# Spreading the residual, two buffers for k by token, and the sample softmax between the projections and the first head

## What is computed

```python
k, v = split(x @ kv_w)                         # (T, 16 heads, 64) each
logf = log_sigmoid(x @ f_w + f_b)              # C = cumulative sum of logf
q = x @ q_w
s = q @ k.T * 64 ** -0.5 + C[t] - C[s]         # causal; softmax, then @ v, then @ o_w
# a sample token attends to 512 cached rows (4 pages of 128) and to itself
x = layer_norm(ALPHA * x + y)
```

## Time and profile before

| | us |
|---|---|
| median of 3 runs | 2961.86 (2959.99 to 2962.94) |
| the profiled execution | 2961.01, its span 2959.3 |
| TensorE busy | 2708.5 (92%) |
| VectorE busy | 1109.4 (37%) |
| GpSimd busy | 949.4 (32%) |
| ScalarE busy | 782.5 (26%) |
| mean granted TensorE clock | 0.942 |

### The profile page before, as it was taken

One profiled execution on the slowest core, in us unless ns is written; L12 is line 12 of the kernel. 1 busy time (PEld: TensorE's weight loads), 2 busy tenths in 40 slices (PEclk: granted clock), 3 DMA queues, 4 the chain that ended last, 5 costly groups with the idle time before them and its releaser, 6 DMA issues.

```text
span 2959.3 us, 44731 instructions
## 1 busy us (share of the span) xinstructions
PE 2708.5 (92%) x16907; PEld 2614.2 (88%) x16907; DVE 1109.4 (37%) x2082; ACT 782.5 (26%) x1431; POOL 949.4 (32%) x546
## 2 busy tenths in 40 slices
PE   8999969999999999679995889889799999999994
PEld 8999949999999999479994688779699999999993
DVE  3222372322222223841236555553623222222237
ACT  2111142111111111522222555552421111111114
POOL 2121252111222121622222778861521112121214
PEclk9999969999999999689997899999799999999997
DMA  3111101111111111024668465641011111111111
GB/s 109 50 43 50 44 15 44 43 44 48 53 47 48 45 50 37 15 85 142 211 216 262 125 172 158 172 138 50 22 44 44 44 57 44 50 44 51 44 36 58
DMA packets 203052, 225.83 MB, mean 76 GB/s; under 512 B 13223, under 2 KB 168871, under 8 KB 201884
## 3 DMA queue, kind: packets, MB, share of 16 engines
q1 hardware_dynamic: 194748, 190.40, 21.2%
q0 software_dynamic: 8160, 33.30, 3.6%
HBM read 182.43 MB, written 41.26 MB: 76 GB/s over the span
## 4 chain that ended last, share of the span: by engine, by line
PE 78%; DVE 7%; DMA 4%; POOL 4%; issue 4%; ACT 2%; SPq 1%; POOLq 0%; ACTq 0%; DVEq 0%
PE ps L1703 24%; PE ps L1704 24%; PE ps L1705 24%; POOL ss L812 2%; PE ps L1961 1%; DMA o_t<-oe 1%; DVE ln_t L1365 1%; PE ps L1991 1%; DVE ln_d L1310 1%; DVE ln_t L1369 1%; PE ps L1946 1%; PE ps L1943 1%; POOL xl L697 1%; DMA k_prompt<-ktok 1%; DMA wraw<-kv_w 1%
## 5 line engine op out<-in xcount | busy, mean ns | idle before, releaser
L1703 PE MATMUL ps<-xh,whi 128*128 128x344 f32 x3288 | 1079.0, 328 | 48.5 <-DVE hl L1512 17.6
L1704 PE MATMUL ps<-xl,whi 128*128 128x344 f32 x3288 | 1063.5, 323 | 0.0
L1705 PE MATMUL ps<-xh,wlo 128*128 128x344 f32 x3288 | 1062.9, 323 | 0.0
L650 POOL TENSOR_TENSOR wlo<-wraw,whi 128x1024 fp32r<-128x1024 f32 x197 | 469.6, 2389 | 1681.5 <-ACT whi L867 1681.4
L1703 PEld LDWEIGHTS ps<-xh,whi 128*128 128x128 f32 x3288 | 626.6, 191 | 79.5 <-POOL xl L697 25.5
L1704 PEld LDWEIGHTS ps<-xl,whi 128*128 128x128 f32 x3288 | 629.6, 191 | 0.0
L1705 PEld LDWEIGHTS ps<-xh,wlo 128*128 128x128 f32 x3288 | 629.3, 191 | 0.0
L867 ACT ACTIVATE whi<-wraw 128x1024 fp32r<-128x1024 f32 x197 | 208.1, 1057 | 1137.6 <-DMA wraw<-ffn_w_gu 648.6
L1703 PE MATMUL ps<-zh,whi 128*128 128x344 f32 x1440 | 464.1, 322 | 17.5 <-DVE x L1437 9.5
L1704 PE MATMUL ps<-zl,whi 128*128 128x344 f32 x1440 | 462.4, 321 | 0.0
L1705 PE MATMUL ps<-zh,wlo 128*128 128x344 f32 x1440 | 460.3, 320 | 0.0
(11 more groups left out here) (209 smaller groups left out, 2374.0 us busy)
## 6 DMA issues: line engine op xcount, KB each, us to landing
wraw<-ffn_w_gu SPq DMA_DIRECT2D x88, 512.0 KB, 3.9
wraw<-ffn_w_down SPq DMA_DIRECT2D x44, 512.0 KB, 3.5
kp<-cache_k SPq DMA_DIRECT2D x32, 512.0 KB, 5.5
vp<-cache_v SPq DMA_DIRECT2D x32, 512.0 KB, 3.8
wraw<-a_w_in SPq DMA_DIRECT2D x24, 512.0 KB, 3.8
wraw<-kv_w SPq DMA_DIRECT2D x16, 512.0 KB, 4.0
q_t<-hl POOLq DMA_DIRECT2D x8, 1024.0 KB, 4.7
v_t<-vst POOLq DMA_DIRECT2D x8, 1024.0 KB, 5.6
```

The source lines that it names most:

```text
L650: pool.tensor_tensor(narrow(wlo[:, s, :], cols), narrow(wraw[:, s, :], cols), f32(narrow(whi[:, s, :], cols)), ALU.subtract).then_inc(w_lo, 1)
L1703: pe.matmul(out, w_h, m_h, start=start, stop=False)
L1704: pe.matmul(out, w_h, m_l, start=False, stop=False)
L1705: return pe.matmul(out, w_l, m_h, start=False, stop=stop)
```

## The change

- The residual moves from one piece ahead of `q_low` to four pieces (`residual(it)`), each behind the second `q_low` of iteration 0 to 3. Three small instructions that prepare the samples' own term (qk, even, side) move ahead of iteration 0.
- k by token gets two buffers, ktok[0] and ktok[1] (the second on the place of `hl`, free after the q stores), with a semaphore each.
- On SyncE the order within iteration 4 to 6 becomes: pages of sample 0, next weight 0, pages of sample 1, next weights 1 and 2. The weights of the output projection go behind `load_qk(0, 0)`, which no longer waits for the last stores; `load_qk(0, 1)` waits for all of them.
- On ScalarE `nxt(1)` goes behind `v_tokens` and `nxt(2)` behind the copies of k by token. The high and low parts of the output projection's first three weights go into attention, behind `step(0, 1)` on ScalarE and behind `norm(0, 3)` on GpSimd.
- On VectorE `v_low` of iterations 4 to 7 goes behind the two samples.
- Iteration 7 is written out on TensorE: the scores of the samples are turned between the two `k_turned` into bank 7, the forget values behind them into bank 0, and `sample_weights` goes behind the first `scores`.
- On GpSimd `k_split(0, 0)` goes ahead of the last two k_prompt stores, and the samples' rows are stored after `norm(0, 0)`.

```diff
-        ktok = ka.put("ktok", [P, TB, P], F32)
+        ktok = [ka.put("ktok0", [P, TB, P], F32), Area(ZH_AT + 3 * ROW + TB * P * 4).put("ktok1", [P, TB, P], F32)]
...
             with sp.Fori(KB // 2, KB - 1) as it:
-                load_kvq(it + 1, True)
-                load_samples(it)
-            for m in range(WR):
-                load(SLOTS["o"] + m, SLOTS["o"] + m, w_o[:, :, m * P:(m + 1) * P], used(UNITS["o"] + m))
-            load_samples(KB - 1)
+                load_sample(it, 0)
+                load_kvq(it + 1, 0, True)
+                load_sample(it, 1)
+                load_kvq(it + 1, 1, True)
+                load_kvq(it + 1, 2, True)
+            load_sample(KB - 1, 0)
+            load_sample(KB - 1, 1)
...
-            sp.wait_ge(full[NCH - 1], UNITS["o"])
             sp.wait_ge(kv["res"], 2 * KB)
             sp.wait_ge(kv["qdma"], 16 * KB)
-            sp.wait_ge(kv["vtdma"], 16 * KB)
-            sp.wait_ge(kv["x0dma"], 16 * (KB // 2))
-            sp.wait_ge(kv["x1dma"], 16 * (KB // 2))
+            sp.wait_ge(kv["vtdma"], 16)
+            sp.wait_ge(kv["x0dma"], 16)
+            sp.wait_ge(full[NCH - 1], UNITS["o"])
             load_qk(0, 0)
             load_v(0, 0)
+            for m in range(WR):
+                load(SLOTS["o"] + m, SLOTS["o"] + m, w_o[:, :, m * P:(m + 1) * P], used(UNITS["o"] + m))
+            sp.wait_ge(kv["vtdma"], 16 * KB)
+            for j in range(2):
+                sp.wait_ge(kv[f"x{j}dma"], 16 * (KB // 2))
+                sp.wait_ge(kv[f"k{j}dma"], 16 * (KB // 2))
             sp.wait_ge(kv["kt"], 4 + 2 * KB)
...
-            keys(KB - 1, lambda j: low(SLOTS["o"] + j, SLOTS["o"] + j))
...
-            pool.dma_start(a["v_sample"].rearrange("b t h d -> b (t h d)"), stok[:, 0, :]).then_inc(kv["s3dma"], 16)
-            pool.dma_start(a["k_sample"].rearrange("b t h d -> b (t h d)"), stok[:, 1, :]).then_inc(kv["s3dma"], 16)
+            store_v(KB - 1)
...
             k_split(0, 0)
+            store_ktok(KB - 1, 0)
+            store_ktok(KB - 1, 1)
             norm(0, 0)
+            sample_rows_out()
             k_split(0, 1)
             for st in range(1, STEPS):
                 norm(0, st)
+            for m in range(WR):
+                low(SLOTS["o"] + m, SLOTS["o"] + m)
...
-                    nxt(1 + j)
                     if j == 0:
                         v_tokens(it)
+                        nxt(1)
                 for j in range(2):
                     if keys:
-                        x = 2 * it + j - KB
-                        if not (isinstance(x, int) and x == 0):
-                            act.wait_ge(kv["kdma"], 16 * x)
-                        by_token(ktok, 5 - 2 * j, kv["kt"], kv["ktok"], 2 * x + 4)
+                        k_tokens(it, j)
+                nxt(2)
+
+            def k_tokens(it, j):
+
+                x = 2 * it + j - KB
+                if isinstance(it, int) and it == KB // 2:
+                    act.wait_ge(kv["qdma"], 16 * KB)
+                else:
+                    act.wait_ge(kv[f"k{j}dma"], 16 * (it - KB // 2))
+                by_token(ktok[j], 5 - 2 * j, kv["kt"], kv["ktok"], 2 * x + 4)
 
             def nxt_slots(it):
                 g = g0 + 3 * it
...
-            kvq(KB - 1, True, nxt_slots(KB - 1))
+            act.wait_ge(kv["vt"], 2 * KB)
+            take(g0 + 3 * (KB - 1), stage[0], 0, KB - 1, 1.0, kv["v"])
+            take_k(KB - 1, 0)
+            v_tokens(KB - 1)
+            take_k(KB - 1, 1)
+            act.wait_ge(sm["tsc"], 1)
+            act.activation(sst[:, 0:NPAST], ps[:, 7, :], ACT.Copy).then_inc(sm["sst"], 1)
+            for j in range(2):
+                k_tokens(KB - 1, j)
 
...
-            act.wait_ge(kv["s3dma"], 16 * 2)
+            act.wait_ge(kv["vtdma"], 16 * KB)
+            for j in range(2):
+                act.wait_ge(kv[f"k{j}dma"], 16 * (KB // 2))
...
             dve.tensor_tensor_scan(fr[:, 0:TP], fz[:, 0:TP], fz[:, 0:TP], 0.0, ALU.add, ALU.bypass).then_inc(kv["f"], 1)
             dve.tensor_tensor(flast[:, :, :], ident[0:H, 0:H].unsqueeze(1).to_broadcast([H, NS, H]),
                               fz[:, TP:T].unsqueeze(2).to_broadcast([H, NS, H]), ALU.mult).then_inc(sm["qk2"], 1)
-            for m in range(KB):
-                dve.tensor_scalar(x32[:, m, :], f32(xh[:, m, :]), ALPHA, None, ALU.mult).then_inc(kv["res"], 1)
-                dve.wait_ge(kv["res"], 2 * m + 1)
-                dve.scalar_tensor_tensor(x32[:, m, :], f32(xl[:, m, :]), ALPHA, x32[:, m, :], ALU.mult, ALU.add).then_inc(kv["res"], 1)
             g0 = UNITS["kvq"]
+
+            def residual(it):
+
+                for m in (2 * it, 2 * it + 1):
+                    dve.tensor_scalar(x32[:, m, :], f32(xh[:, m, :]), ALPHA, None, ALU.mult).then_inc(kv["res"], 1)
+                    dve.wait_ge(kv["res"], 2 * m + 1)
+                    dve.scalar_tensor_tensor(x32[:, m, :], f32(xl[:, m, :]), ALPHA, x32[:, m, :], ALU.mult, ALU.add).then_inc(kv["res"], 1)
 
...
                     low.then_inc(kv["vl"], 1)
 
-            with dve.Fori(0, KB // 2) as it:
+            dve.wait_ge(const_done, 11)
+            dve.memset(qk[:, :, :, :], 0.0).then_inc(sm["qk"], 1)
+            dve.tensor_reduce(even[:, :], ident[:, :].rearrange("p (j t) -> p t j", t=2), AX, ALU.add).then_inc(sm["even"], 1)
+            dve.wait_ge(sm["even"], 1)
+            dve.tensor_copy(side[:, :].rearrange("p (t d) -> p t d", t=2), even[:, :].unsqueeze(2).to_broadcast([P, 2, DH])).then_inc(sm["even"], 1)
+            dve.wait_ge(sm["qk"], 1)
+            for it in range(KB // 2):
                 q_low(it, 0)
                 v_low(it)
                 q_low(it, 1)
+                residual(it)
 
 
...
-
-
-            dve.wait_ge(const_done, 11)
-            dve.memset(qk[:, :, :, :], 0.0).then_inc(sm["qk"], 1)
-            dve.tensor_reduce(even[:, :], ident[:, :].rearrange("p (j t) -> p t j", t=2), AX, ALU.add).then_inc(sm["even"], 1)
-            dve.wait_ge(sm["even"], 1)
-            dve.tensor_copy(side[:, :].rearrange("p (t d) -> p t d", t=2), even[:, :].unsqueeze(2).to_broadcast([P, 2, DH])).then_inc(sm["even"], 1)
-            dve.wait_ge(sm["qk"], 1)
+                v_low(it + KB // 2)
+
+
             dve.wait_ge(kv["x"], 2 * KB)
...
                 pe.wait_ge(kv["rowq"], 1)
+
+            with pe.Fori(KB // 2, KB - 1) as it:
+                keys(it)
                 for j in range(2):
                     k_turned(it, j)
...
-            pe.wait_ge(kv["ktok"], 2 * KB)
-            sample_rows(0, 5)
-            pe.wait_ge(kv["ktok"], 2 * KB + 2)
-            sample_rows(1, 3)
-
...
+            keys(KB - 1)
+            k_turned(KB - 1, 0)
+            pe.wait_ge(kv["ftok"], 2)
             pe.wait_ge(sm["sc"], NS * PPB + PPB)
             for g in range(PPB):
-                mm = pe.transpose(ps[:, 4, g * P:(g + 1) * P], sc[:, g, :], ident[:, :])
+                mm = pe.transpose(ps[:, 7, g * P:(g + 1) * P], sc[:, g, :], ident[:, :])
             mm.then_inc(sm["tsc"], 1)
+            k_turned(KB - 1, 1)
+            for c in range(NCH):
+                pe.wait_ge(free[c], UNITS["o"])
             pe.wait_ge(sm["lgd"], 16 * NS * PPB)
             for g in range(PPB):
...
-
+            pe.wait_ge(sm["sst"], 1)
...
+            sample_rows(0, 1)
+            pe.wait_ge(kv["ktok"], 2 * KB)
+            sample_rows(1, 5)
+
+            def sample_weights():
+
+                pe.wait_ge(sm["pn"], 1)
+                pe.wait_ge(kv["rowk"], 1)
+                for g in range(PPB):
+                    mm = pe.transpose(ps[:, 6, g * P:(g + 1) * P], sst[:, g * P:(g + 1) * P], ident[:, :])
+                mm.then_inc(sm["pt"], 1)
+                pe.wait_ge(sm["pn"], 2)
+                pe.matmul(ps[:, 7, SCOL:SCOL + KB * NS], side[:, :], pnew[:, :, :].rearrange("p k b -> p (k b)"),
+                          start=True, stop=True).then_inc(sm["pe"], 1)
...
-                pe.wait_ge(free[c], UNITS["o"])
-            pe.wait_ge(kv["ftok"], 2)
-            pe.wait_ge(sm["sst"], 1)
-            pe.wait_ge(sm["pst"], 1)
+            pe.wait_ge(sm["slf"], 1)
+            pe.wait_ge(kv["rowv"], 1)
             for st in range(3):
                 for t in range(2):
                     scores(0, st, t)
+                if st == 0:
+                    sample_weights()
```

77 lines of the change are left out of this document (40 added, 37 removed).

## The result

The change takes 2908.95 us (2905.37 to 2915.53) where the kernel before takes 2962.4: a ratio of 0.982 with a 95% interval of 0.980 to 0.984. The forecast was 2907 us. The profiled execution is 2906.83 us, its span 2905.2, so the two profiled spans differ by 54.1 us against a sum of 54.7. One execution of a later kernel (more work for GpSimd) took 8004.12 us and is left out of every figure.

The account below looks back on a forecast made before the run. TensorE is busy 92% of the span, so only standstills and slow stretches can be gained: 14.2 - 6.3 + 15.6 + 33.8 - 2.6 = 54.7 us off 2961.0, forecast 2907 us, own range 2900 to 2914, range with rivals 2895 to 2920.

Parts of the forecast that it names:

- Residual: Ahead of iteration 0: TensorE's 17.6 us wait for hl shrinks to 3.4 us, saving 14.2 us; 0 to 2.6 more possible.
- Pages ahead of weight 0: Iteration 4: weight 0 issued at 20.3 us behind pages; TensorE waits 3.7 us plus 2.6 of clock, 6.3 us lost.
- the 2.6 us of clock: Clock loss added to each TensorE standstill of a few us from full speed, here in iteration 4.
- k iterations 5 and 6: Both iterations lose their waits and take 36.9 us each, 15.6 us gained.
- Into the second attention step: From iteration 7's start to step 1's transposes: 68.8 us instead of 102.6, 33.8 us gained, held by head 1's load.
- the rival of crowded DMAs: Head 0's load takes 14.2 us instead of 8.6 beside other transfers, shifting all behind it 5.6 us: 2913 us, chance 0.15.
- Low parts in attention: Three output-weight low parts, 7.2 us on GpSimd between norm(0, 3) and norm(0, 4), lose 2.6 us; bounds 0 and 7.2.

Follow-up runs that it names:

- more work for GpSimd: Changed kernel with three more GpSimd instructions (8.25 us) ahead of the output weights' low parts in the first head pair: 2915.35 us, 0.9846 of the kernel before.
- the turned one: Changed kernel with GpSimd issuing both k_prompt stores first, then both head splits, first norm, samples' rows last: 2907.06 us, 0.9808 of the kernel before.
- the third experiment: Kernel before plus two k-by-token buffers and the new k-iteration orders, without the residual move or new way into attention: 2930.74 us, 0.989.

## Why the prediction was right, and where its terms were off

**Residual: right.** 14.7 us of the wait went (17.62 to 2.94), forecast 14.2. From the v transposes of iteration 0 to those of iteration 1 it was 15.6 us less, so another 0.9 us is clock: behind the short wait the clock was down for some 3 us (rows in the last section), where it had been 0.50 over 5 us. The bounds of 0 to 2.6 held, and the experiment with this part alone gave some 16, good to 5.

**Pages ahead of weight 0: right in place, too large.** Forecast 6.3 us, measured 2.9: iteration 4 took 39.84 us (1406.97 to 1446.81) against 36.92. The weight was issued at 19.0 us into the iteration, not 20.3, and its high part began 4.6 us later, not 5.5. So the wait for stage was 1.22 us instead of 3.7. A second one of 1.52 us for `v_low` came behind it, which the prediction had put at nothing, since the unit was to be later than `v_low`; it did add. The step that failed is the 2.6 us of clock: behind waits of 1.22 and 1.52 us no matmul ran at half clock. I had added that to each standstill of a few us, from one row of 5.6 us. For standstills of that size the 2.6 holds: 7.4 us of iteration 6 before are a wait of 4.8 and 2.6 more, and with weight 0 first waits of 4.3 to 5.2 us cost 1.4 to 2.5 more. Moving the weight ahead, which looks like the cure, costs 10 to 14 us, since it delays the pages of three iterations to save those 2.9.

**k iterations 5 and 6: right.** 37.0 us each, forecast 36.9. The experiments show that the buffer alone is not enough, since 8.8 us of waits for stage stay with it, and that the buffer with the new orders is; which of the orders are needed was not run.

**Into the second attention step: right within 1 us as a sum, within 2 us step by step.** Iteration 7 began at 1520.81, 37.0 us behind the start of the one before. Scores began 49.0 us into it (forecast 47.1), the second split 63.5 (62.4), turn 1 69.8 (68.8). 1.6 of the 1.9 us at the first step are head 0's load, which took 10.2 us, not 8.6, and not the 14.2 of the rival of crowded DMAs. A part of that rival came true, and it is no fixed one: in the seven profiles with this order on GpSimd the load took 9.9 to 12.6 us. Then 0.5 us was made good: the second k_prompt store, issued at about 1570.5, landed by 1575.77, in 5.3 us and not 5.8. Head 1's load took 8.6 us as put.

**Low parts in attention: right in sign, a little small.** Forecast 2.6 us. With them in the first pair turn 1 to page unit 4 takes 45.2 to 47.8 us, without them 42.1 to 43.9; by the means it is 3.5 us more in the change's GpSimd order and 3.9 in the turned one. The extra 8.25 us gave 9, so no cover was left, as the step had it. That their removal doesn't show in the times is no evidence against it, as the loop behind them varies by more. The milestone itself moves by 1.3 us between two profiles of one kernel.

**What cancelled.** Against the sum: pages 3.4 us better, residual 1.4 better, k iterations 0.2 worse (15.4 us), the way into attention 1.0 worse, low parts 1.8 worse (46.5 against 42.1 us in this pair of profiles; by the means about 1), with 1.1 given back in the loop behind them (307.2 against 308.3, so the later steps of attention took the time that they took before). And ahead of the stage the profiled execution of after was 3.3 us later than that of before (first v transposes at 1283.36 instead of 1280.06), in code that the change does not touch; over all 14 profiles here these transposes begin at 1280.1 to 1286.0 us. So the hit to 2 us is partly luck; the terms were good to 3.4 us or better each.

**The part that I had not asked.** The softmax's 10.7 us in the third experiment brought 5 us. 3.5 us of the others are the low parts, which that kernel did not have in attention; the rest, 1 to 2 us, lies within what the loop of attention varies by. The 5 is a difference of times that are good to 5 us each, so this is a sum that fits and not one that is shown.

## What to carry to other kernels

When a wait on one engine is removed, list what each queue on the way still holds in its order; here the second buffer alone gave a third of what it gave together with the orders of loads and of VectorE. Where the DMA share was 1.0 here, moving a transfer moved most of the delay to another waiter: look at each load in the new profile, and at which engine then waits last, before the gain is booked. And to judge a part of 3 us in a kernel of 2900, compare two milestones around it instead of total times.
